# The last two groups of both token mixers in another order, and the first mixer's chunks joined

## The chip, the cores and the metric

The kernel runs on one core of one Trainium2 chip. Its engines are TensorE (PE; its weight loads are listed as PEld), VectorE (DVE), ScalarE (ACT), GpSimd (POOL) and the queue of SyncE (SP), from which most transfers are issued. Each engine works through its own list of instructions in order and waits on semaphores. The metric is the time of one execution in microseconds (us).

## The reference, cut to what matters

The trunk has two layers on 256 tokens of width 1024: SwiGLU feed-forward, token mixer, SwiGLU feed-forward, each between two RMS norms. The mixer of layer 0 is gated linear attention (GLA, 4 heads), that of layer 1 is the Mamba-2 mixer (SSD, 8 groups). All is float32.

```python
def rmsnorm(x, g):
    y = x * lax.rsqrt(mean(x * x, -1) + 1e-6)
    return y * g

for i in range(2):
    x = x + 0.5 * rmsnorm(swiglu(rmsnorm(x, g[0]), ...), g[1])
    h = rmsnorm(x, g[2])
    h = gla_mixer(h, ...) if i == 0 else ssd_mixer(h, ...)
    x = x + rmsnorm(h, g[3])
    x = x + 0.5 * rmsnorm(swiglu(rmsnorm(x, g[4]), ...), g[5])

# gla_mixer, per head, chunks of 64 tokens; b = cumulative log decay in the chunk
scores = tril(einsum(q * exp(b - b_mid), k * exp(b_mid - b)))
o_i    = scores @ v + (q * exp(b)) @ state
state  = state * exp(b_last) + (k * exp(b_last - b)).T @ v
o      = rmsnorm(o per head, g_norm) * silu(r); return o @ w_out

# ssd_mixer, per group: causal conv of 4 taps and silu on x, B, C; chunked scan in the same manner,
y      = (y + d * x) * silu(z); y = rmsnorm(y per group of 256, g_norm); return y @ w_out
```

## The kernel before, in words

**Matrix products.** Each float32 weight is split into a high part, rounded to the format fp32r, and the rest. ScalarE makes the high part (`hi`, and `gate_up_hi` for a quarter of a feed-forward unit, lines 527 and 577), VectorE the rest (`lo`, `gate_up_lo`, lines 891 and 975): 2048 columns on 128 partitions for a mixer's weight slot, 1024 for a quarter. A product is then three TensorE passes. Products of plain float32 tiles (transposes, scores, state) go through TensorE without a split.

**Memory.** Four weight slots (0 to 3) take the transfers; slots 0 and 1 also hold a feed-forward unit's gate and up weights, in four quarters. PSUM has eight banks: 0 to 3 collect the output of the stage (two token tiles of 128 by 1024 columns), A, B, C and E (4 to 7) are working banks.

**A mixer** runs over its groups (heads in GLA) in a software pipeline of three steps, `body(g, proj, scan, outp)` on each engine: *proj* projects group g (P1: features, P2, P3: tokens), *scan* computes group g-1 (rows of keys transposed, scores, state, output, norm), *outp* multiplies the normed output of group g-2 with its rows of `w_out` into banks 0 to 3 (`add_output`, 24 products of 512 columns). The loop runs g = 2 to n-2, and `body(n-1)`, `body(n)` and `body(n+1)` are written out. `body(n)` projects nothing: it scans the last group. `body(n+1)` only adds the last group's output. There the next feed-forward stage's first unit is converted too: all four quarters stand in `body(n-1)`.

**A group's norm** (line 1310 on): ScalarE squares and sums, VectorE computes 1/root in 13 small steps by shift and three Newton iterations (`rsqrt2`, line 900; one more product before and after in GLA), scales `yn` (line 1325), TensorE transposes it (line 1620), ScalarE takes it out of PSUM (line 809) and VectorE its rest (line 1223), and `add_output` can start.

**GLA** has four chunks of 64: three state products on 64 rows (line 1701), four products of the scores (line 1721), three with the states (line 1727), between them a copy and two updates of the state on VectorE (lines 1267 and 1270). `decayed` (line 1136) makes the decayed queries and keys, each by one operation of 256 columns. SSD already works on tiles of 128 tokens.

**The boundary** behind a mixer: each half of the output (512 columns) is squared on ScalarE (line 546) and multiplied with the gains on VectorE (line 927), then the root, the residual update (line 945), TensorE's transposes of x (line 1404) and the first products of the feed-forward stage (line 1362). GpSimd multiplies SSD's rows with their weights (lines 490 to 498).

## Time and profile before

| | us |
|---|---|
| median of 3 runs | 1189.26 |
| lowest and highest run | 1186.78, 1190.22 |
| the profiled execution, its own time | 1189.44 |
| its span, first to last instruction | 1187.7 |
| TensorE busy | 1123.2 (95%) |
| VectorE busy | 738.4 (62%) |
| ScalarE busy | 631.4 (53%) |
| TensorE's mean granted clock | 0.969 of full |

TensorE is busy nearly always. A reader looks for the stretches in which it is not, and for the stretches in which its granted clock is half. GLA lies at 227 to 357 us of the span, SSD at 751 to 995.

### The profile page before, as it was taken

Reading aid. Unit: us, or ns where it says so; the run is one execution under the profiler, and the core shown is the slowest. Engines: PE = TensorE matmul, PEld = TensorE weight load, DVE = VectorE, ACT = ScalarE, POOL = GpSimd, SP = SyncE. Lnnn points to the kernel's source line nnn. Section 1 sums busy time; section 2 is a strip of 40 time slices with the busy share of each in tenths; the row PEclk is TensorE's granted clock in tenths of the full one; section 3 lists DMA queues with packets and bytes.
Section 4 is the critical chain, followed back from the end, with each engine's and each line's share of the span. In section 5 each row is a group of like instructions: output and inputs, shape, how many; then the busy total and the mean of one; then the engine's idle time right before and its main releaser. Section 6 shows DMA issues by size and latency. Waiting matters only on the chain. (4 is left out here: it accounts for less than half of the span.)

```text
span 1187.7 us, 16534 instructions
## 1 busy us (share of the span) xinstructions
PE 1123.2 (95%) x5904; PEld 950.9 (80%) x5904; DVE 738.4 (62%) x1174; ACT 631.4 (53%) x978; POOL 52.2 (4%) x81
## 2 busy tenths in 40 slices
PE   6899999969979999999999997999999969999997
PEld 5688888858848888888888885889999957888886
DVE  4545555756657555557655545698999885655554
ACT  6444445664437444447544445577677746544443
POOL 3000000000000000000000000211211100000000
PEclk9899999989979999999999998899999978999999
DMA  7756554443445655553766534484544504855530
GB/s 244 248 178 211 183 170 133 134 134 115 142 142 175 223 178 176 184 190 118 250 203 198 177 106 137 155 272 144 172 144 143 176 15 147 282 192 177 176 127 35
DMA packets 162877, 199.24 MB, mean 168 GB/s; under 512 B 6372, under 2 KB 145856, under 8 KB 162832
## 3 DMA queue, kind: packets, MB, share of 16 engines
q1 hardware_dynamic: 160144, 190.34, 49.4%
q0 software_dynamic: 2384, 7.72, 1.9%
q8 instruction: 26, 0.43, 0.2%
q10 hardware_dynamic: 304, 0.61, 0.1%
q14 instruction: 19, 0.16, 0.0%
HBM read 197.56 MB, written 1.08 MB: 167 GB/s over the span
## 5 line engine op out<-in xcount | busy, mean ns | idle before, releaser
L1362 PE MATMUL ps<-ws,xT 128*128 128x512 f32 x2160 | 502.3, 391 | 6.2 <-DVE ws L979 6.2
L1362 PEld LDWEIGHTS ps<-ws,xT 128*128 128x128 f32 x2160 | 404.6, 188 | 93.8 <-DVE ws L979 8.0
L1381 PE MATMUL ps<-ws,hT 128*128 128x512 f32 x1344 | 337.8, 402 | 4.0 <-DVE hT L1223 3.9
L1381 PEld LDWEIGHTS ps<-ws,hT 128*128 128x128 f32 x1344 | 253.5, 192 | 59.1 <-issue 6.8
L979 DVE TENSOR_TENSOR ws<-raw,ws 128x1024 fp32r<-128x1024 f32 x180 | 218.3, 1223 | 117.1 <-ACT ws L592 116.9
L897 DVE TENSOR_TENSOR ws<-raw,ws 128x2048 fp32r<-128x2048 f32 x90 | 206.8, 2298 | 99.1 <-ACT ws L532 98.7
L592 ACT ACTIVATE ws<-raw 128x1024 fp32r<-128x1024 f32 x180 | 188.3, 1060 | 145.3 <-PE ps L1362 141.7
L532 ACT ACTIVATE ws<-raw 128x2048 fp32r<-128x2048 f32 x90 | 171.1, 1913 | 58.6 <-PE ps L1381 52.4
L1414 PE MATMUL ps<-xT,ws 128*128 128x256 f32 x960 | 119.3, 284 | 0.3 <-ACT feat L538 0.3
L1414 PEld LDWEIGHTS ps<-xT,ws 128*128 128x128 f32 x960 | 116.4, 192 | 0.9 <-DVE ws L897 0.5
L992 DVE TENSOR_TENSOR hT<-ps,hT 128x256 fp32r<-128x256 f32 x88 | 33.7, 420 | 87.0 <-ACT hT L606 86.9
L1424 PE MATMUL ps<-ws,xT 128*128 128x256 f32 x672 | 87.4, 291 | 0.4 <-ACT ca L538 0.4
L1424 PEld LDWEIGHTS ps<-ws,xT 128*128 128x128 f32 x672 | 84.6, 197 | 2.9 <-issue 2.1
L606 ACT ACTIVATE hT<-ps 128x256 fp32r<-128x256 f32 x88 | 29.5, 381 | 100.4 <-PE ps L1373 100.3
L601 ACT ACTIVATE fm<-ps,sm 128x256 f32<-128x256 f32 x88 | 41.2, 474 | 57.8 <-PE ps L1362 57.8
L985 DVE SCALAR_TENSOR_TENSOR fm<-ps,sm,fm 128x256 f32<-128x256 f32 x88 | 41.8, 483 | 31.9 <-ACT fm L601 31.6
L1156 DVE SCALAR_TENSOR_TENSOR ca<-feat,pcol,ca 128x256 f32<-128x256 f32 x96 | 49.6, 583 | 0.0
L507 POOL DMA_DIRECT2D gpost<-in_norm_gain x5 | 2.8, 556 | 756.1 <-DVE scr L927 756.1
L538 ACT ACTIVATE feat<-ps 128x256 f32<-128x256 f32 x32 | 12.0, 382 | 41.6 <-PE ps L1414 41.3
L927 DVE TENSOR_TENSOR scr<-ps,gpost 128x512 f32<-128x512 f32 x24 | 16.6, 691 | 28.0 <-ACT scr L546 28.0
L969 DVE SCALAR_TENSOR_TENSOR xT<-ps,gcol,xT 128x128 fp32r<-128x128 f32 x96 | 26.6, 343 | 11.6 <-ACT xT L574 11.1
L574 ACT ACTIVATE xT<-ps,gcol 128x128 fp32r<-128x128 f32 x96 | 26.3, 375 | 12.0 <-PE ps L1404 12.0
(196 smaller groups left out, 632.8 us busy)
## 6 DMA issues: line engine op xcount, KB each, us to landing
raw<-in_ffn_w_down SPq DMA_DIRECT2D x88, 512.0 KB, 4.3
raw<-in_ffn_w_gate SPq DMA_DIRECT2D x86, 512.0 KB, 4.0
raw<-in_ffn_w_up SPq DMA_DIRECT2D x86, 512.0 KB, 5.0
raw<-in_ssd_w_in SPq DMA_DIRECT2D x48, 512.0 KB, 4.7
raw<-in_gla_w_in SPq DMA_DIRECT2D x24, 512.0 KB, 4.7
raw<-in_ssd_w_out SPq DMA_DIRECT2D x16, 512.0 KB, 4.2
raw<-in_gla_w_out SPq DMA_DIRECT2D x8, 512.0 KB, 4.8
exps<-cs_rows POOLq DMA_DIRECT2D x8, 512.0 KB, 8.9
```

Source lines behind the costliest of these rows:

```text
L532: act.activation(ws[:, slot, 0, :], raw[:, slot, :], ACT.Copy).then_inc(hi_done[slot], 1)
L592: act.activation(ws[:, 0:2, 0, c], raw[:, 0:2, c], ACT.Copy).then_inc(gu_hi, 1)
L601: act.activation(fm[:, t, :], ps[:, bank + t, 0:UW], ACT.Silu, scale=RPRE[t]).then_inc(silu_g, 1)
L897: return dve.tensor_tensor(ws[:, slot, 1, cols], raw[:, slot, cols], ws[:, slot, 0, cols].bitcast(F32), ALU.subtract)
L979: dve.tensor_tensor(ws[:, 0:2, 1, c], raw[:, 0:2, c], ws[:, 0:2, 0, c].bitcast(F32), ALU.subtract).then_inc(gu_lo, 1)
L985: dve.scalar_tensor_tensor(out=fm[:, 2 + t, :], in0=ps[:, bank + t, UW:2 * UW], scalar=RPRE[t], in1=fm[:, t, :], op0=ALU.mult, op1=ALU.mul ...
L992: dve.tensor_tensor(hT[:, par, :, 1, cs], ps[:, C + t, 0:T].rearrange("p (j n) -> p j n", j=2), hT[:, par, :, 0, cs].bitcast(F32), ALU.sub ...
L1156: ins = dve.scalar_tensor_tensor(out=ca[:, c, :], in0=src, scalar=tap, in1=ca[:, c, :], op0=ALU.mult, op1=ALU.add)
L1362: mm = pe.matmul(ps[:, bank + t, :].rearrange("p (s n) -> p s n", s=2), xT[:, k, a, t * P:(t + 1) * P], ws[:, 0:2, b, k * UW:(k + 1) * UW] ...
L1381: mm = pe.matmul(ps[:, 2 * t + n, :], hT[:, par, j, a, t * P:(t + 1) * P], ws[:, slot, b, off:off + 512], start=(first and j + a + b == 0) ...
L1414: mm = pe.matmul(ps[:, banks + c, 0:T], ws[:, slot, a, off:off + P], xT[:, k, b, :], start=(k == 0 and a + b == 0), stop=(k == KD - 1 and ...
L1424: mm = pe.matmul(ps[:, banks + t, 0:UW], xT[:, k, a, t * P:(t + 1) * P], ws[:, slot, b, k * UW:(k + 1) * UW], start=(k == 0 and a + b == 0 ...
```

## The change

On every engine `body(n-1)`, `body(n)` and `body(n+1)` of both mixers are reordered.

- TensorE: the last group's P3 is cut in two tiles; between them stand the transposed rows and the scores of the last group, which stood in `body(n)`. The first tile's bank stays C, the second's is A, the scores go to B. `add_output` of group n-2 is one piece of 24 products in front of the last transposes, where it was two of 12.
- ScalarE: the four quarters leave `body(n-1)`. Two stand in `body(n)` ahead of the second P3 tile's evacuation, two behind the conversion of the last output weights. The table for Sqrt is loaded in `body(n)`, behind the last Silu, and the last group's root is taken by ScalarE.
- VectorE: the quarters leave `body(n-1)`; three stand behind the last group's transposed rest, the fourth in the boundary. SSD's second convolution stands ahead of the state's copy, and the output weights of group n-2 are converted ahead of the norm (in SSD). The last group's 1/root is a reciprocal of ScalarE's root with one Newton iteration.
- GLA's chunks are joined in all groups: two chunks make a tile of 128 tokens, the decay between them is folded into `decayed` (three operations instead of one for two of the four features), and a group has one state product, two products of the scores on 128 rows and one with the state.

In SSD, TensorE's end before, from the last group's P3 (ws by xT, 256 columns) to the output's products ahead of the transposes of x:

```order
L1424 MATMUL ps<-ws,xT 128x256 x48
L1647 MATMUL ps<-ident,fm 128x128 x4
L1665 MATMUL ps<-ident,fm 128x128
L1668 MATMUL ps<-fm 128x128 x2
L1620 MATMUL ps<-ident,yn 128x128 x4
L1696 MATMUL ps<-xw,scr 128x256
L1712 MATMUL ps<-xdt,wm 128x64 x8
L1716 MATMUL ps<-scr,fm 128x256
L1381 MATMUL ps<-ws,hT 128x512 x12
L1620 MATMUL ps<-ident,yn 128x128 x4
L1381 MATMUL ps<-ws,hT 128x512 x30
```

and now:

```order
L1476 MATMUL ps<-ws,xT 128x256 x24
L1684 MATMUL ps<-ident,fm 128x128 x4
L1693 MATMUL ps<-ident,fm 128x128
L1696 MATMUL ps<-fm 128x128 x2
L1476 MATMUL ps<-ws,xT 128x256 x24
L1674 MATMUL ps<-ident,yn 128x128 x4
L1762 MATMUL ps<-xw,scr 128x256
L1775 MATMUL ps<-xdt,wm 128x64 x8
L1779 MATMUL ps<-scr,fm 128x256
L1433 MATMUL ps<-ws,hT 128x512 x24
L1674 MATMUL ps<-ident,yn 128x128 x4
L1433 MATMUL ps<-ws,hT 128x512 x18
```

The transposed rows of `fm` and the scores stand between two halves of P3, and `add_output` (ws by hT) of group n-2 is whole in front of the last transposes of `yn`; behind them 18 products stand ahead of the transposes of x, where 30 stood.

In SSD, VectorE before, from the state's copy in `body(n-1)`, and then the scaling of `yn` there:

```order
L1247 COPY scr<-ps 128x256
L979 TENSOR_TENSOR ws<-raw,ws 128x2x512 x2
L1153 TENSOR_SCALAR ca<-feat,pcol 128x256 x2
L1156 SCALAR_TENSOR_TENSOR ca<-feat,pcol,ca 128x256 x6
L1288 TENSOR_TENSOR yn<-ps,dx 128x512
L1290 TENSOR_TENSOR vs<-ps,dtv 128x256
L1293 TENSOR_TENSOR yn<-yn,vs 128x256
L1295 TENSOR_TENSOR yn<-yn,zs 128x512
L979 TENSOR_TENSOR ws<-raw,ws 128x2x512 x2
...
L1325 TENSOR_SCALAR yn<-yn,sm 128x256 x2
L897 TENSOR_TENSOR ws<-raw,ws 128x2048
```

and now, from the decayed scores in `body(n-1)`, and then the last scaling and what follows it:

```order
L1311 TENSOR_TENSOR wm<-exps,scr 128x512 x2
L1188 TENSOR_SCALAR ca<-feat,pcol 128x256 x2
L1191 SCALAR_TENSOR_TENSOR ca<-feat,pcol,ca 128x256 x6
L1320 COPY scr<-ps 128x256
L1354 TENSOR_TENSOR yn<-ps,dx 128x512
L1356 TENSOR_TENSOR vs<-ps,dtv 128x256
L1359 TENSOR_TENSOR yn<-yn,vs 128x256
L1361 TENSOR_TENSOR yn<-yn,zs 128x512
L918 TENSOR_TENSOR ws<-raw,ws 128x2048
...
L1275 TENSOR_SCALAR yn<-yn,sm 128x256 x2
L1291 SCALAR_TENSOR_TENSOR hT<-ps,pcol,hT 128x256 x2
L1000 TENSOR_TENSOR ws<-raw,ws 128x2x512 x3
```

The quarters (128x2x512) are gone from between the convolution, the output and its norm; three follow the last transposed rest. The convolution (`ca`) moved ahead of the copy.

In GLA's loop, TensorE's products behind P2 before (`xw`: state, `wm`: scores by values, `fm` and `scr`: queries by states):

```order
L1673 MATMUL ps<-fm 64x64 x4
L1381 MATMUL ps<-ws,hT 128x512 x24
L1701 MATMUL ps<-vs,xw 128x256 x3
L1721 MATMUL ps<-vs,wm 64x256 x4
L1727 MATMUL ps<-scr,fm 64x256 x3
```

and now:

```order
L1701 MATMUL ps<-fm 64x64 x4
L1704 MATMUL ps<-fm 64x64 x2
L1433 MATMUL ps<-ws,hT 128x512 x24
L1766 MATMUL ps<-vs,xw 128x256
L1783 MATMUL ps<-vs,wm 128x256 x2
L1786 MATMUL ps<-scr,fm 128x256
```

Ten products became four, the scores six instead of four.

In the diff `ahead` is `body(n-1)` and `tail` is `body(n)`; `p3_tile(o, t, bank)` evacuates one P3 tile on ScalarE.

```diff
...
-                        act.activation(bcb[:, :], ps[:, C, 0:384], ACT.Copy).then_inc(e_out, 1)
-                    if scan and not proj:
-                        transposed(A)
-                    if isinstance(g, int) and g == n - 1:
-                        for q in range(NQ):
+                        act.activation(bcb[:, :], ps[:, B if tail else C, 0:384], ACT.Copy).then_inc(e_out, 1)
+                    if tail:
+                        for q in range(2):
                             gate_up_hi(gate_units_before(ph + 1), q, ph + 1)
-                    elif proj:
+                        p3_tile(n - 1, 1, A)
+                        if ssd:
+                            gate_silu()
+                        act.activation(DUMMY, EPS_COL[1.0], ACT.Sqrt)
+                        transposed(C)
...
                         hi(*out_unit(g - 1, n, n0))
+                    if tail:
+                        for q in range(2, NQ):
+                            gate_up_hi(gate_units_before(ph + 1), q, ph + 1)
...
+                    if tail:
+                        act.wait_ge(y_sq, 2 * (g - 1 + G) + 2)
+                        for t in range(NT):
+                            act.activation(sm[:, 26 + t:27 + t], sm[:, 8 + t:9 + t], ACT.Sqrt, scale=1.0 if ssd else R2[:, t:t + 1],
+                                           bias=EPS_COL[1.0 / 16]).then_inc(root_y, 1)
...
+                if b < NPH and PHASES[b - 1][0] != "ffn":
+                    gate_up_lo(gate_units_before(b), NQ - 1)
...
+                    near, far, through = (3, 0, 2) if o == 2 else (0, 3, 1)
+                    step.start(part(o, far * CH, near * CH, CH))
+                    part(o, CH, CH, 2 * CH)
+                    step.wait()
+                    dve.tensor_scalar(fm[:, o, near * CH:(near + 1) * CH], fm[:, o, far * CH:(far + 1) * CH],
+                                      edl[:, 0, bass.ds(4 * g + through, 1)], None, ALU.mult).then_inc(feat_done, 1)
...
+                        dve.wait_ge(root_y, 4 if ssd else 2)
+                        step(dve.reciprocal(y, sm[:, 26:28]))
+                        step(dve.tensor_tensor(a, y, y, ALU.mult))
+                        step(dve.tensor_tensor(a, a, mh, ALU.mult))
+                        step(dve.scalar_tensor_tensor(out=y, in0=a, scalar=1.5, in1=y, op0=ALU.add, op1=ALU.mult))
...
+                    if not scan:
+                        for q in range(NQ - 1):
+                            gate_up_lo(gate_units_before(ph + 1), q)
...
-                        for c, (bank, o) in () if ssd else ((0, (E, 0)), (2, (E, 256)), (1, (C, 0))):
...
+                            pe.matmul(ps[:, E, 0:256], xw[:, 0, 0:P], vs[:, 0, :], start=True, stop=True,
+                                      skip_group_check=True).then_inc(upd_mm, 1)
+                        if tail:
+                            pe.wait_ge(p3_out, 2 * (g - 1 + G) + 2)
...
+                            for t in range(NT):
+                                pe.matmul(ps[:, A + t, 0:256], wm[:, t, 0, :], vs[:, t, :], start=True, stop=(t == 0),
                                           skip_group_check=True)
...
+                            pe.wait_ge(state_done, g)
+                            pe.matmul(ps[:, B, 0:256], fm[:, 2, P:2 * P], st[:, 0, :], start=False, stop=True,
+                                      skip_group_check=True).then_inc(off_mm, 1)
+                    if tail:
+                        add_output(n - 2)
+                    if ahead:
+                        split(SLOT_P3, g + n0[SLOT_P3])
+                        pe.wait_ge(state_done, G + g if ssd else g)
+                        token_tiles(SLOT_P3, C, (0,))
+                        pe.wait_ge(feat_done, 4 * (g + G) + 2)
+                        rows(g)
+                        pe.wait_ge(y_out, 2 * (g - 1 + G) + 2)
+                        scores(g, B)
+                        token_tiles(SLOT_P3, A - 1, (1,))
...
```

## Rows read from the trace of the kernel before

**Rows 1.** TensorE's waits: line, releaser: us in total, times, longest.

```profile
PE ps L1620 <- DVE yn L1325: 11.8, 3, 4.7
PE ps L1649 <- DVE fm L1140: 8.6, 1, 8.6
```

**Rows 2.** TensorE in order of time, SSD's end: start us, us, form [idle before].

```profile
950.77 6.09 PE L1424 MATMUL ps<-ws,xT 128*128 128x256 f32 x48
...
964.30 1.11 PE L1620 MATMUL ps<-ident,yn 128*128 128x128 f32 x4 [4.65 <-DVE yn L1325]
...
980.48 0.66 PE L1620 MATMUL ps<-ident,yn 128*128 128x128 f32 x4 [3.38 <-DVE yn L1325]
983.07 9.78 PE L1381 MATMUL ps<-ws,hT 128*128 128x512 f32 x30 [1.93 <-DVE hT L1223]
...
994.94 5.08 PE L1362 MATMUL ps<-ws,xT 128*128 128x512 f32 x21
```

**Rows 3.** Windows 328.1:334.7, 341.7:348.3, 959.5:973.0, 980.0:986.7: length, busy per engine, clock, DMA.

```profile
959.50:973.00 13.50, 6.20 (x27) 5.27 (x25) 9.07 (x19) 3.31 (x5) 2.75 (x4) 0.57 0.00 1
...
sum 33.40, PE 18.21 PEld 13.40 DVE 17.25 ACT 11.31 POOL 2.75; mean PE 4.55 PEld 3.35 DVE 4.31 ACT 2.83 POOL 0.69
```

**Rows 4.** TensorE in order of time, SSD's loop undisturbed.

```profile
862.28 5.73 PE L1381 MATMUL ps<-ws,hT 128*128 128x512 f32 x24
867.85 0.59 PE L1696 MATMUL ps<-xw,scr 128*128 128x256 f32 x2
868.28 1.89 PE L1712 MATMUL ps<-xdt,wm 128*128 128x64 f32 x16
```

**Rows 5.** TensorE in order of time, GLA's third group and the stage's end.

```profile
317.24 1.13 PE L1701 MATMUL ps<-vs,xw 64*128 64x256 f32 x6
...
320.63 6.01 PE L1424 MATMUL ps<-ws,xT 128*128 128x256 f32 x48
...
357.43 5.09 PE L1362 MATMUL ps<-ws,xT 128*128 128x512 f32 x21
```

**Rows 6.** The page's costliest groups: busy us, mean ns | idle before.

```profile
L979 DVE TENSOR_TENSOR ws<-raw,ws 128x1024 fp32r<-128x1024 f32 x180 | 218.3, 1223 | 117.1 <-ACT ws L592 116.9
L897 DVE TENSOR_TENSOR ws<-raw,ws 128x2048 fp32r<-128x2048 f32 x90 | 206.8, 2298 | 99.1 <-ACT ws L532 98.7
L592 ACT ACTIVATE ws<-raw 128x1024 fp32r<-128x1024 f32 x180 | 188.3, 1060 | 145.3 <-PE ps L1362 141.7
```

**Rows 7.** VectorE in order of time: loop norm, then the last two groups.

```profile
932.15 0.16 DVE L903 TENSOR_SCALAR sm<-sm 128x2 f32<-128x2 f32 x1
...
934.58 0.61 DVE L1325 TENSOR_SCALAR yn<-yn,sm 128x256 f32<-128x256 f32 x2
...
954.45 0.69 DVE L1288 TENSOR_TENSOR yn<-ps,dx 128x512 f32<-128x512 f32 x1
...
959.03 0.16 DVE L903 TENSOR_SCALAR sm<-sm 128x2 f32<-128x2 f32 x1
...
963.63 0.62 DVE L1325 TENSOR_SCALAR yn<-yn,sm 128x256 f32<-128x256 f32 x2 [0.28 <-DVE sm L912]
```

**Rows 8.** GpSimd in order of time, the last group.

```profile
959.81 0.61 POOL L490 TENSOR_TENSOR xw<-scr,dtv 128x256 f32<-128x256 f32 x1 [19.08 <-ACT scr L818]
```

**Rows 9.** VectorE in order of time: GLA's state and features, the boundary's residual update.

```profile
318.93 1.06 DVE L1270 SCALAR_TENSOR_TENSOR scr<-scr,edl,ps 128x256 f32<-128x256 f32 x2
319.92 1.09 DVE L1140 SCALAR_TENSOR_TENSOR fm<-ca,exps 128x256 f32<-128x256 f32 x3
...
990.65 1.42 DVE L945 SCALAR_TENSOR_TENSOR xres<-scr,sm,xres 128x512 f32<-128x512 f32 x2
```

**Rows 10.** ScalarE in order of time behind GLA's last group.

```profile
345.24 1.28 ACT L614 ACT_TABLE_LOAD   x1
346.54 0.20 ACT L614 ACTIVATE sm<-sm 128x1 f32<-128x1 f32 x1
```

**Rows 11.** The page's DMA issues: KB each, median us to landing.

```profile
raw<-in_ffn_w_up SPq DMA_DIRECT2D x86, 512.0 KB, 5.0
```

More of the change, by code:

```diff
@@ L36 @@
 QW = UNIT // NQ
-CONST_IDENT, CONST_EPS, CONST_ALL = 2, 5, 12
+CONST_IDENT, CONST_EPS, CONST_ALL = 2, 6, 12
 SSD_WEIGHTS = 4
-SSD_STEPS, GLA_STEPS = 15, 15
+SSD_STEPS, GLA_STEPS = 15, 17
 MASKED_FIRST = 2
@@ L466, in _ @@
             step(pool.memset(ones[:, :], 1.0))
-            for c in range(2):
-                r = slice(c * CH, (c + 1) * CH)
-                step(pool.tensor_copy(mask[r, :], tri[r, r]))
+            step(pool.memset(wm[CH:P, :, 0, 0:CH], 0.0))
             step(pool.memset(feat[:, :, 0:CONV - 1], 0.0))
@@ L788, in body, with gate_silu @@
                     first = isinstance(g, int) and g == 1
-                    if scan:
+                    ahead = isinstance(g, int) and g == n - 1
+                    tail = scan and not proj
+                    def gate_silu():
                         if not first:
@@ L1215, in body @@
                     first = isinstance(g, int) and g == 1
+                    ahead = isinstance(g, int) and g == n - 1
+                    tail = scan and not proj
                     c0 = g * 2 + 2 * G
@@ L1248, in body @@
                         else:
-                            mk = mask[:, :].rearrange("p (t i) -> p t i", t=1).broadcast_to([P, NT, CH])
                             dve.wait_ge(e_mm, g - 1 + G + 1)
-                            dve.tensor_tensor(wm[:, :, 0, 0:CH], ps[:, C, 0:P].rearrange("p (t i) -> p t i", t=2), mk,
-                                              ALU.mult).then_inc(w_done, 2)
-                    if scan and not proj:
-                        transposed(A)
-                    if isinstance(g, int) and g == n - 1:
-                        for q in range(2):
-                            gate_up_lo(gate_units_before(ph + 1), q)
-                    elif proj:
+                            scores = ps[:, B if tail else C, 0:2 * P].rearrange("p (t i) -> p t i", t=2)
@@ new lines, in body @@
+                            past = tri[:, CH:P].rearrange("p (t i) -> p t i", t=1).broadcast_to([P, NT, CH])
+                            dve.tensor_tensor(wm[:, :, 0, CH:P], scores[:, :, CH:P], past, ALU.mult).then_inc(w_done, 1)
+                            past = tri[0:CH, 0:CH].rearrange("p (t i) -> p t i", t=1).broadcast_to([CH, NT, CH])
+                            dve.tensor_tensor(wm[0:CH, :, 0, 0:CH], scores[0:CH, :, 0:CH], past, ALU.mult).then_inc(w_done, 1)
+                    if tail and not ssd:
+                        transposed(C)
@@ L1605, in body @@
                     last = not proj and not scan
+                    ahead = isinstance(g, int) and g == n - 1
+                    tail = scan and not proj
                     c0 = g * 2 + 2 * G
@@ L1679, in body @@
                         add_output(n - 1, (0,), True)
-                        add_output(n - 2, (1,))
                         add_output(n - 1, (1,), True)
-                    if scan and not proj:
-                        transpose_rows(A)
+                    if tail:
+                        pe.wait_ge(p3_out, 2 * (g - 1 + G) + 1)
+                        transpose_rows(C)
                     if scan:
```

186 lines of the change are left out of this document (99 added, 87 removed).

## The prediction

> **What bounds the kernel now.** Start with the busy shares: TensorE 95%, the others far below. So TensorE's list sets the time, and only three things can shorten it: fewer or shorter products, fewer waits, fewer stretches at half clock. The view of TensorE's waits comes next. The reader is to see that two of its rows are nearly half of all that TensorE waits: the transposes of `yn` behind the norm, 11.8 us in 3 waits, and the transposes in front of GLA's first scan, 8.6 us once [rows 1]. Then the list in order of time shows where the first sits: at SSD's end. From the last P3 (950.77) to the feed-forward stage's first product (994.94) 44.2 us pass, with waits of 4.65, 3.38 and 1.93 us [rows 2], of which some 6.1 us are P3 itself. GLA's end looks the same: 317.24 to 357.43, 40.2 us [rows 5]. Last the windows: in the four stretches where the waits lie, the granted clock is 0.57 in the longest, that is mostly the lower level of 1.2 GHz, and TensorE is busy 18.21 us in the 33.4 [rows 3]. The same four transposes take 1.11 us at 964.30 and 0.66 at 980.48 [rows 2]: what is half clocked takes nearly twice as long. These two ends are the place of the change.
>
> **SSD's end, walked step by step.** Up to 950.77 TensorE does the same work in the same order.
> - P3's first tile takes half of 6.09 us, to 953.8; transposed rows and scores about 0.9 (a guess from neighbours of 128 columns), the second tile to 957.6.
> - VectorE: the convolution ran ahead of the copy, in time in which it waited, and two quarters of 1.22 us [rows 6] are gone. So the output starts not at 954.45 but when TensorE's product is there, 950.8: 3.7 us earlier, done at 953.2. Then a conversion of 2.3 us [rows 6], and the norm starts at 955.4 instead of 959.03.
> - The norm. In the loop it takes 934.58 + 0.61 - 932.15 = 3.0 us; in the last groups 963.63 + 0.62 - 959.03 = 5.2 us [rows 7]. The difference of 2.2 us begins with GpSimd's multiplies at 959.81 [rows 8], and VectorE's small steps stretch while they run. In the new order GpSimd gets its rows at about 955.1, so its multiplies again fall on the norm. I take 5.1: done at 960.5. TensorE waits 2.9 us, where it waited 4.65. Without the overlap it would be 0.8.
> - The decayed scores (1.3) come behind the norm on VectorE, to 961.8; then the scores' product 1.9 and the state's 0.4, to 964.0; `add_output` in one piece, 5.7 [rows 4], to 969.7.
> - Beside it: output to gated output 2.4 us from 963.8, squares 0.8, roots and five small steps 1.5, two scalings 0.6, and the conversion of 2.3 us in between, partly hiding squares: 970.0. TensorE waits 0.3 where it waited 3.38. The remaining transposes, ScalarE's copy and VectorE's rest take 983.07 - 980.48 = 2.6 us [rows 2] as before: 972.6.
> - Then 12 + 6 products to 976.9. Here is the new wait. The residual update of the first tile must be done before TensorE transposes x. Before, 30 products (7.2 us at full clock, 9.78 as granted) covered it; now only 6 stand between the tile's end at 975.5 and the transposes. Squares, gains, root chain, half an update of 1.42 us [rows 9] and the three quarters of 3.7 us in front of the gains put x at 979.0. Wait: 2.1 us. Transposes and 6 products end at 981.7.
> - 994.94 - 981.7 = **13.2 us saved** at full clock. The fourth quarter (1.2 us) falls where VectorE waits for the second tile's squares; I cost it at 0, or 1.2 if that cover is gone.
>
> **GLA's end.** The same list from 317.24: products 1.7 instead of 3.4 (below), first tile, rows and scores, second tile to 325.6. The norm (3.4 us here) no longer has quarters ahead and is done at 324.7, so TensorE doesn't wait for it. New waits come: ScalarE loads the Sqrt table (1.28 us [rows 10]) behind the second tile's evacuation, so the transposed copy starts at 327.7, not 326.1; and the masked scores stand behind a conversion on VectorE, 327.6. TensorE waits 1.5 us there and 1.0 for the state copied behind the rest of `hT`. `add_output` ends at 336.05; ScalarE converts two quarters of 1.06 us [rows 6] ahead of the squares, and the norm is still done at 335.7. Then 2.4, 12 + 6 products, 2.5 for x, and the end at 347.7. 357.43 - 347.7 = **9.7 us saved** at full clock.
>
> **GLA's loop.** Ten products took 320.63 - 317.24 = 3.39 us [rows 5]. The new four are of the form 128x256 on 128 rows, whose start-to-start is 868.28 - 867.85 = 0.43 us [rows 4]: 1.72. That is 1.7 less per group; the two added score products (64x64) about pay for the dropped transpose. Groups 1 and 2 give **3.4** (bounds 2.0 and 4.0: the first group also waits on VectorE), group 3 is in the walk above. VectorE loses two state updates of 0.53 and gains steps in `decayed`: three features took 1.09, 0.36 each [rows 9]; three pieces with a wait cost at least three small ones of 0.16 [rows 7] and at most three of 0.36, so +0.15 to +0.75 each. I take +0.3. In the loop TensorE covers that; at GLA's start two of these stand ahead of the products that already wait 8.6 us [rows 1]: **-0.6** (0.3 to 1.5). The masks' replacement on GpSimd lies in the first microseconds: 0.
>
> **The clock.** Both walks assume 2.4 GHz. In the four windows TensorE was busy 18.21 us [rows 3], so the lower level cost up to 9.1. New waits of 1 to 3 us remain at five places, so the clock will still fall. Lower bound 0, upper 12 (a denser list at half clock loses more per us). I take **-6**, nearer to before, since the 2.9, 2.1 and 2.6 us waits resemble those that led to a fall.
>
> **Sum.** 13.2 + 9.7 + 3.4 - 0.6 - 6 = 19.7. The profiled execution took 1189.44 (span 1187.7, 1.7 outside); the median of the runs is 1189.26, the same within 0.02%. 1189.44 - 19.7 = **1169.7 us**.
>
> **A rule weighed against the change.** GLA's new table load lies on the path. In the trace it takes 1.28 us, from 345.24, and the next instruction starts at 346.54, 0.02 behind it [rows 10]; 1.28 is what the walk holds. The Trainium skill, ScalarE: Activation LUTs, "What ACT_TABLE_LOAD costs", adds to each switch of tables a drain of about 1.4 us. By that rule the gain would be 1.4 us smaller, 1171.1; this trace shows no such gap.
>
> **Rivals.**
> - *The clock stays up.* If the closed waits keep it at 2.4 GHz nearly everywhere, the 6 us come back: 1164. For it: 3.38 and half of 4.65 us of waits go at SSD's end; against: waits remain in both ends.
> - *New waits take more.* The residual update that lost its cover (18 instead of 30 products), the fourth quarter, the Sqrt load and the norm that still meets GpSimd each cost more than walked, about 1.5 us each in two stages, and the clock costs 9 instead of 6. Then 10 to 11 us are left: 1179. For it: each is a chain over three engines that I pieced together; against: each is short.
> - *The waits only move.* If the reordered ends gave nothing but the freed products and the first wait, 3.4 + 1.7 + 3 = 8 minus new ones of 4: 1185. Against: the norm's earlier start rests on order alone.
> - *Slower: the next stage starves.* The loads of the second feed-forward unit into slots 0 and 1 wait for the first unit's converted quarters, and these now end at about 348.8 in GLA's walk (347.7 and the fourth quarter's 1.2), where they stood in `body(n-1)`. With 5.0 us to land [rows 11] the second unit is there at 354, and ScalarE wants it when TensorE has read the first unit's first quarters, some 10 us behind 347.7. From 3 us more it decides: if the late transfers queued so that each stage's start waits over 10 us, both together eat the gain: 1192. Nothing in the trace shows such a landing time.
>
> **How the numbers follow.** Forecast (1166 to 1174) 0.45; clock stays up 0.2; new waits take more 0.24; waits only move 0.06; starving 0.05. The likeliest is 1169.7. The range for 8 in 10 takes most of the second and third: 1161 to 1179. A difference of 0.3% (3.6 us) is about what a measurement of this kernel can tell from none. Faster by more than that: 0.92 (all but the last and part of the fourth); within: 0.04; slower: 0.04.
>
> **What would show it.** Right: the wait of the `yn` transposes falls from 11.8 to about 3.2 us, all in SSD; the time from SSD's last P3 to the first feed-forward product is 31 us plus the clock's loss; GLA's loop step falls by 1.7 per group; the transposes of x wait about 2 us at both ends. Wrong: the norm done before 959 (no meeting with GpSimd), waits of over 4 us ahead of the transposes of x, half clock over more than 20 us in the two ends, or waits for raw weights in the first units.

## The result, and the profile of the changed kernel

The changed kernel takes 1168.41 us (median of 4 runs, 1166.21 to 1170.95), the kernel before 1189.74 in the same session (1186.78 to 1190.90): 0.9821 of the time, 95% interval 0.9804 to 0.9838, so 21.3 us less. The prediction said 1169.7. The profiled execution is the shortest of the four, 1166.21 us with a span of 1164.5 (the span runs from the first instruction to the last); its span is 23.2 us shorter than the one before, and that is the sum to be split.

TensorE's waits, largest and new ones (line, releaser: us in total, times, longest), beside [rows 1]:

```profile
PE ps L1686 <- DVE fm L1176: 9.0, 1, 9.0
...
PE ps L1433 <- DVE hT L1291: 3.9, 2, 1.9
...
PE ps L1456 <- DVE xres L966: 3.2, 2, 1.6
PE ps L1674 <- DVE yn L1275: 2.4, 1, 2.4
PE ps L1786 <- DVE scr L1336: 2.4, 2, 1.3
```

The transposes of `yn` waited 11.8 us in three places and now wait 2.4 in one. New are 3.2 us ahead of the transposes of x, in two waits. The wait at GLA's start is 9.0 instead of 8.6.

TensorE in order of time at SSD's end, beside [rows 2]:

```profile
937.47 3.21 PE L1476 MATMUL ps<-ws,xT 128*128 128x256 f32 x24
...
946.98 0.63 PE L1674 MATMUL ps<-ident,yn 128*128 128x128 f32 x4 [2.44 <-DVE yn L1275]
947.44 0.60 PE L1762 MATMUL ps<-xw,scr 128*128 128x256 f32 x2
948.09 3.68 PE L1775 MATMUL ps<-xdt,wm 128*128 128x64 f32 x16
951.56 1.17 PE L1779 MATMUL ps<-scr,fm 128*128 128x256 f32 x2
952.16 7.13 PE L1433 MATMUL ps<-ws,hT 128*128 128x512 f32 x24
959.13 0.60 PE L1674 MATMUL ps<-ident,yn 128*128 128x128 f32 x4
961.66 5.95 PE L1433 MATMUL ps<-ws,hT 128*128 128x512 f32 x18 [1.93 <-DVE hT L1291]
969.17 1.32 PE L1456 MATMUL ps<-ident,xres 128*128 128x128 f32 x8 [1.56 <-DVE xres L966]
...
971.70 5.11 PE L1414 MATMUL ps<-ws,xT 128*128 128x512 f32 x21
```

From the last P3 to the feed-forward stage's first product 34.23 us pass where 44.17 did: 9.94 gained. Of these 8.3 are waits: before there were five, the three of [rows 2] and these two, 14.21 us together, and now three of 5.93 us.

```profile
958.47 0.63 PE L1647 MATMUL ps<-ident,fm 128*128 128x128 f32 x4 [1.60 <-ACT zf L538]
...
968.92 3.65 PE L1712 MATMUL ps<-xdt,wm 128*128 128x64 f32 x16 [2.65 <-DVE hT L1223]
```

The 16 products at 948.09 take 3.68 us, against 1.89 at full clock [rows 4], and the 18 at 961.66 take 5.95: behind the waits of 2.44 and 1.93 us TensorE runs at half clock. At GLA's end the kernel before had these four waits, 8.24 us in all:

```profile
327.29 0.41 PE L1649 MATMUL ps<-ident,fm 128*128 128x128 f32 x2 [0.66 <-ACT vs L538]
...
330.60 2.04 PE L1701 MATMUL ps<-vs,xw 64*128 64x256 f32 x6 [1.83 <-DVE wm L1251]
...
343.42 0.93 PE L1620 MATMUL ps<-ident,yn 128*128 128x128 f32 x4 [3.82 <-DVE yn L1325]
346.28 9.06 PE L1381 MATMUL ps<-ws,hT 128*128 128x512 f32 x30 [1.93 <-DVE hT L1223]
```

And now, beside [rows 5]:

```profile
314.38 0.59 PE L1766 MATMUL ps<-vs,xw 128*128 128x256 f32 x2
...
322.77 0.60 PE L1674 MATMUL ps<-ident,yn 128*128 128x128 f32 x4
324.38 0.67 PE L1766 MATMUL ps<-vs,xw 128*128 128x256 f32 x2 [1.01 <-DVE wm L1327]
...
326.98 0.70 PE L1786 MATMUL ps<-scr,fm 128*128 128x256 f32 x2 [1.07 <-DVE scr L1336]
...
335.53 4.36 PE L1433 MATMUL ps<-ws,hT 128*128 128x512 f32 x18 [1.93 <-DVE hT L1291]
341.53 1.32 PE L1456 MATMUL ps<-ident,xres 128*128 128x128 f32 x8 [1.64 <-DVE xres L966]
...
344.07 2.21 PE L1414 MATMUL ps<-ws,xT 128*128 128x512 f32 x9
```

29.69 us instead of 40.19: 10.50 gained, and here the 18 products take 4.36 us, full clock. The waits explain only 2.6 of it (5.65 us now). The other 7.9 are shorter products: some 3.4 are the joined chunks' in the third and the last group (an estimate, 3.39 us for ten products before, 1.54 and 1.88 for four now), and most of the rest is half clock that is gone (the 30 products behind 346.28 took 9.06 us, 7.2 at full clock). The granted clock of this stretch was 0.83 before and is 1.00 now; SSD's end had 0.77 and has 0.85.

The third group starts at 314.38 instead of 317.24, 2.86 earlier: 2.64 of it lie between GLA's first products and there, and 0.22 ahead of them, where TensorE's list is the same in both kernels. 9.94 + 10.50 + 2.86 = 23.3 of the 23.2 us. The two windows (length, busy us per engine, TensorE's clock, DMA), GLA's end and SSD's:

```profile
314.40:344.00 29.60, 23.95 (x142) 19.97 (x141) 23.64 (x67) 18.48 (x40) 0.00 (x0) 1.00 0.31 107
```
```profile
937.50:971.70 34.20, 28.21 (x143) 23.89 (x142) 26.58 (x58) 18.88 (x43) 2.85 (x4) 0.85 0.26 93
```

VectorE's norm in SSD's last full group (first and last step), and GpSimd beside it:

```profile
941.98 0.58 DVE L924 TENSOR_SCALAR sm<-sm 128x2 f32<-128x2 f32 x1
...
946.22 0.62 DVE L1275 TENSOR_SCALAR yn<-yn,sm 128x256 f32<-128x256 f32 x2
```
```profile
941.83 0.71 POOL L488 TENSOR_TENSOR xw<-scr,dtv 128x256 f32<-128x256 f32 x1 [14.41 <-ACT scr L827]
942.50 1.04 POOL L491 TENSOR_TENSOR xdt<-scr,dtv 128x512 f32<-128x512 f32 x1
```

The norm still meets GpSimd's multiplies and takes 4.86 us, not the loop's 3.0 [rows 7].

### The profile page after: what moved, and what is told of

It reads as the page before. It is cut to its first block, busy times and chain, and to the rows that moved or that the text cites. A ratio compares the mean times of both kernels' runs of the same rounds, so it can differ in the third digit from the quotient of the medians.

```text
span 1164.5 us, 16442 instructions
## 1 busy us (share of the span) xinstructions
PE 1111.0 (95%) x5868; PEld 947.5 (81%) x5868; DVE 733.4 (63%) x1170; ACT 631.9 (54%) x984; POOL 54.1 (5%) x81
## 4 chain that ended last, share of the span: by engine, by line
PE 88%; DVE 6%; ACT 3%; issue 1%; DMA 1%; SPq 0%; DVEq 0%; ACTq 0%
PE ps L1414 41%; PE ps L1433 25%; PE ps L1466 8%; PE ps L1476 6%; PE ps L1425 2%; PE ps L1775 1%; DVE ws L918 1%; DVE ws L1000 1%; PE ps L1456 1%; ACT ws L530 1%; DMA raw<-in_ffn_w_down 1%; PE ps L1584 1%; DVE xT L990 1%; DVE xres L966 0%; DVE ca L1191 0%
## 5 line engine op out<-in xcount | busy, mean ns | idle before, releaser
L1425 PE MATMUL ps<-ident,fm 128*128 128x128 f32 x176 | 27.6, 276 | 3.2 <-DVE fm L1006 3.2
```

Of the source, the lines that this page charges most:

```text
L1425: mm = pe.transpose(ps[:, C + t, j * P:(j + 1) * P], fm[:, 2 + t, j * P:(j + 1) * P], ident[:, :])
```

## The experiments

Twelve kernels, each timed beside the kernel before (medians 1189.47 to 1189.74). Single runs of one kernel spread over 2 to 7 us and the intervals of the ratios are 1.5 to 2.6 us to each side, so a difference of less than some 2 us between two of these medians says little; the traces decide there. "SSD's end" and "GLA's end" are the two stretches above.

Whole traces can't be compared either. TensorE reaches GLA's first product with `xdt` at 228.53 us in one of these traces and at 233.51 in another (229.95 before, 229.73 in the changed kernel), although its list is the same to there; the granted clock of the first 60 us was 0.94 and 0.83 in these two. The time from GLA's end to SSD's last P3, the same list too, goes from 590.64 to 594.72 us (593.34 and 593.40). Behind SSD's end all of them take 192.7 to 192.8. So only the two ends are compared below.

**The joined chunks alone.** In the kernel before:

```diff
-                        for c, (bank, o) in () if ssd else ...
+                            for to, keys, queries in ((CH, 3, 1), (3 * CH, 2, 0)):
+                                mm = pe.matmul(ps[0:CH, C, to:to + CH], fm[:, 3, keys * CH:(keys + 1) * CH], ...
+                            pe.matmul(ps[:, E, 0:256], xw[:, 0, 0:P], vs[:, 0, :], start=True, stop=True, ...
```

> The kernel before with one part of the change alone: GLA's chunks joined (one state product per group of 256 tokens, one output product more per tile, no transpose of the second feature tile). Theory: the joined chunks give back 1.5 to 1.7 us in each of two groups of the loop, 1.3 in the last group at full clock and somewhat more where that ran at half clock, less 0.6 at GLA's start: 4.5 to 6 us, about 1184. Then the order of the last groups and the norm hold the other 15 to 17 us. Rival: in the kernel before, the added VectorE steps of the features are not covered and the freed TensorE time turns into waits at the norm: 0 to 2 us, 1187 to 1190. A second rival, that the clock alone reacts (a denser list keeps it up in GLA's end): over 7 us, under 1182.

1184.65 us, ratio 0.9947 (0.9934 to 0.9960): 5.1 us less. GLA's end shrank from 40.19 to 36.75, more than its share of products, SSD's hardly (44.17 to 43.46). The waits at `yn` stayed, in four places:

```profile
PE ps L1621 <- DVE yn L1326: 11.6, 4, 4.4
```

So the join gives about 5 us, and the other 16 are the order's by subtraction: no run has the order without the join.

**The quarters back in the last full group.**

```diff
+                    if ahead:
+                        for q in range(NQ):
+                            gate_up_hi(gate_units_before(ph + 1), q, ph + 1)
...
+                    if ahead:
+                        for q in range(2):
+                            gate_up_lo(gate_units_before(ph + 1), q)
...
+                    if ahead:
+                        for q in range(2, NQ):
+                            gate_up_lo(gate_units_before(ph + 1), q)
...
-                        for q in range(NQ - 1):
-                            gate_up_lo(gate_units_before(ph + 1), q)
```

> The changed kernel with one part undone: the feed-forward weights' quarters are converted in the last full group again, two on VectorE and all four on ScalarE ahead of the norm, as before the change. Theory: in SSD's end the norm starts about 2.4 us later (two quarters of 1.22 us), and all of it reaches TensorE, since it waits 2.4 us there already; GLA's norm has 1.2 us of slack. ScalarE loses the quarters behind the last norm and the boundary gains a little. Together +3 to +5 us with what the longer wait costs in clock: 1171.5 to 1173.5. Rival: the norm meets GpSimd's multiplies in the present order and takes 4.9 instead of 3.0 us; a later norm misses them, so only 0.5 us is lost: 1169. In that case the norm's duration in the trace is near 3 us. Second rival: the loads behind the quarters start earlier and something is gained, below 1167.

1171.42 us, 0.9839 (0.9826 to 0.9852): 3.0 more than the changed kernel. TensorE's waits:

```profile
PE ps L1673 <- DVE yn L1271: 5.0, 3, 3.7
```

SSD's end is 37.29 us (939.59 to 976.88), 3.06 longer; the norm takes 4.8 us again, so the first rival is out. GLA's end is 32.18 us, 2.5 longer: the norm is late there too (1.13), the masked scores are (1.96 instead of 1.01), and the products behind run at half clock. The two ends together are 5.55 us longer in the traces; the medians differ by 3.0, and the intervals of the ratios just overlap (the changed kernel's ends at 0.9838). The conversions did stand in front of the norm. It is the only piece of the order that, undone alone, cost a measurable time: the next two runs undo one each and their medians don't differ. The remaining 13 us or so (the rows and scores brought ahead into `body(n-1)`, the convolution ahead of the copy, `add_output` in one piece) rest on the traces' waits and clock; no run takes them apart.

**The last root on VectorE.**

```diff
-                    if tail:
-                        act.wait_ge(y_sq, 2 * (g - 1 + G) + 2)
...
-                        norm(g, tail)
+                        norm(g, False)
```

> The changed kernel with the last norm's root computed on VectorE by steps, as in the loop, and no root on ScalarE; the load of the Sqrt table stays where it is. Theory: the last norm is on the path with little slack (SSD: yn ready at 958.05, TensorE there at 959.13; GLA: 332.4 against 333.0). The chain on VectorE is about 1.5 to 1.9 us longer than root, reciprocal and four steps, so each end loses 0.5 to 1.3 us: +1 to +2.5 us, 1169.5 to 1171. Rival: VectorE's chain is hidden behind the second conversion or ScalarE's squares, as TensorE waited for another thing there: no change, 1168.4 within 0.5. The wait of the transposes of yn in the third place tells them apart.

1168.56 us, 0.9812 (0.9798 to 0.9827): no difference in time. The waits do appear, 0.53 us in SSD's end and 0.88 in GLA's:

```profile
961.27 0.66 PE L1669 MATMUL ps<-ident,yn 128*128 128x128 f32 x4 [0.53 <-DVE yn L1270]
963.86 4.36 PE L1428 MATMUL ps<-ws,hT 128*128 128x512 f32 x18 [1.93 <-DVE hT L1286]
```

In SSD the 18 products behind run at full clock here (4.36 against 5.95 us), which outweighs the wait: 33.34 instead of 34.23. In GLA's end it is the other way round:

```profile
338.36 5.95 PE L1428 MATMUL ps<-ws,hT 128*128 128x512 f32 x18 [1.93 <-DVE hT L1286]
```

GLA's end is 32.29 us where it was 29.69, 0.88 for the wait and 1.6 for the clock. The step is worth up to 1.4 us of waits, about as much as one such change of the clock (1.6).

**P3 in one piece ahead of rows and scores.**

```diff
                         token_tiles(SLOT_P3, C, (0,))
+                        pe.wait_ge(y_out, 2 * (g - 1 + G) + 2)
+                        token_tiles(SLOT_P3, A - 1, (1,))
                         pe.wait_ge(feat_done, 4 * (g + G) + 2)
                         rows(g)
-                        pe.wait_ge(y_out, 2 * (g - 1 + G) + 2)
                         scores(g, B)
-                        token_tiles(SLOT_P3, A - 1, (1,))
```

> The changed kernel with both tiles of P3 in one piece in the last full group of SSD and GLA, and the transposed rows and scores behind them instead of between them. Theory: rows and scores come 3 us later, so ScalarE's token copy, GpSimd's multiplies and the masked scores on VectorE come later as well; TensorE gains nothing ahead of the norm, and the scores' product waits about 1 to 2 us longer in each end: +1.5 to +4 us, 1170 to 1172.5. Rival: GpSimd's multiplies then fall behind VectorE's norm, which takes 3.0 instead of 4.9 us, and TensorE's wait of 2.4 us at the first yn transposes shrinks: -1 to -2 us, 1166.5 to 1167.5. The norm's duration and the wait ahead of the state product tell them apart.

1168.67 us, 0.9830 (0.9816 to 0.9844): not to be told from the changed kernel. Both mechanisms are there. In SSD's end GpSimd now falls behind the norm, which takes 3.0 us (942.16 to 945.2), and the first wait shrinks; two others take its place:

```profile
945.35 0.63 PE L1674 MATMUL ps<-ident,yn 128*128 128x128 f32 x4 [0.61 <-DVE yn L1275]
947.27 0.67 PE L1762 MATMUL ps<-xw,scr 128*128 128x256 f32 x2 [1.29 <-POOL xdt L491]
...
951.70 1.22 PE L1779 MATMUL ps<-scr,fm 128*128 128x256 f32 x2 [0.59 <-DVE scr L1320]
```

0.61 + 1.29 + 0.59 = 2.49 for 2.44. SSD's end is 34.14 us, as long as before this edit. GLA's end is 32.48, 2.8 longer: the state's copy comes later (2.33 us of wait in place of 1.07), as the theory had it for each end, and the last 18 products run at half clock (5.97).

**Zeros in the waits.** They add 0 to a bank and change no result.

```diff
+                        for _ in range(count):
+                            pe.matmul(ps[:, 3, :].rearrange("p (o n) -> p o n", o=4), zr[:, :], zeros, start=False, ...
...
+                        fill(8 if ssd else 3)
                         pe.wait_ge(p3_out, 2 * (g - 1 + G) + 1)
...
                         transpose_rows(C)
+                        if last:
+                            fill(6)
...
+                                fill(5)
                                 x_transposed(ph + 1, 0)
```

> The changed kernel with products of zeros added in TensorE's waits at both ends of the mixers: 3 (GLA) or 8 (SSD) ahead of the first yn transposes of the last part, 6 behind the last yn transposes, 5 ahead of the transposes of x. They add zeros into a bank of PSUM with the form 128x512 of the output products, so each takes 0.24 us at full clock. Theory: after SSD's waits TensorE runs for some 7 and 3 us at the lower level of 1.2 GHz, which costs about 3.3 us in SSD's end in the trace of the changed kernel; zeros in the waits keep the level up and this comes back: -2 to -3.5 us, 1165 to 1166.5, with granted clock 1.0 in SSD's end. Rival: the level falls for another reason than TensorE's pause, or the zeros reach beyond the waits and push the path: no gain or +1 us.

1163.95 us, 0.9779 (0.9764 to 0.9795): 4.5 less than the changed kernel, more than the theory's 3.5. SSD's end:

```profile
947.94 2.01 PE L1682 MATMUL ps<-zr 128*128 128x512 f32 x8
950.55 0.63 PE L1674 MATMUL ps<-ident,yn 128*128 128x128 f32 x4 [0.60 <-DVE yn L1275]
...
951.66 2.00 PE L1786 MATMUL ps<-xdt,wm 128*128 128x64 f32 x16
...
953.79 5.84 PE L1433 MATMUL ps<-ws,hT 128*128 128x512 f32 x24
959.83 0.66 PE L1674 MATMUL ps<-ident,yn 128*128 128x128 f32 x4 [0.20 <-DVE yn L1275]
...
962.42 4.35 PE L1433 MATMUL ps<-ws,hT 128*128 128x512 f32 x18 [0.55 <-DVE hT L1291]
```
```profile
941.10:970.90 29.80, 27.90 (x162) 23.13 (x161) 26.32 (x58) 18.85 (x43) 2.85 (x4) 1.00 0.30 106
```

The norm ends no earlier (9.37 us behind the start of P3 in both), the other engines do the same, and yet the stretch is 29.92 us instead of 34.23: 3.68 becomes 2.00, 7.13 becomes 5.84, 5.95 becomes 4.35. A wait of 0.20 us at the last transposes takes a little back, and 4.31 us are what half clock cost in SSD's end. GLA's end is 29.71 us against 29.69, as it was at full clock already. The Trainium skill, TensorE: Matmul & The Clock Gate, "What's actually happening", says that the clock depends on how busy the array has been lately, and the trace agrees: the clock was 1.00 with the waits filled, 0.85 without. It isn't an accident of one run: in SSD's end the clock is 1.00 in all three kernels with zeros, and 0.85 to 0.95 in the nine with the new order and no zeros.

**Six output products moved behind the last transposes.**

```diff
-                        add_output(n - 2)
+                        add_output(n - 2, (0,))
+                        down_half(out_unit(n - 2, n, n0)[0], 0, 1, 0)
...
                         transpose_rows(C)
+                        if last:
+                            down_half(out_unit(n - 2, n, n0)[0], 0, 1, 1)
```

> The changed kernel with 6 of the 24 output products of the group before the last moved behind the last yn transposes in both mixers, where TensorE waits 1.93 us for hT. Theory: each of these waits is filled with 1.45 us of products; in front, yn becomes ready 1.1 us (SSD) and 0.6 us (GLA) ahead of TensorE's arrival, so 0.35 and 0.9 us are lost again to a new wait at the transposes: -1.1 and -0.6, together about -1.5 us, 1166.5 to 1167.5. Rival: the wait only moves to the transposes of yn and of x (the end hangs on VectorE's chain, not on TensorE's list): 1168 to 1169. The sum of the waits at yn, hT and xres tells them apart.

1164.42 us, 0.9786 (0.9771 to 0.9801): 4.0 less, more than either expectation. The waits at `hT` fall from 1.93 to 0.55 us; in SSD's end (31.70 us, 2.5 less) that also keeps the last 18 products at full clock, 4.37 us. GLA's end is 29.24, where a wait of 0.69 at `yn` came. The 16 and the first 18 products behind SSD's wait of 2.44 us still run mostly at half clock (3.59 and 5.87 us; 2.00 and 4.47 in the run with both edits below).

**Norm ahead of the conversion.**

```diff
-                        act.activation(DUMMY, EPS_COL[1.0], ACT.Sqrt)
                         transposed(C)
+                        act.activation(DUMMY, EPS_COL[1.0], ACT.Sqrt)
...
                             if tail:
+                                lo(*out_unit(g - 2, n, n0))
                                 transposed(C)
...
-                    if ssd and scan and not first and (ahead or tail):
+                    if ssd and tail:
                         lo(*out_unit(g - 1, n, n0))
...
-                    if scan and proj and not (ssd and ahead):
+                    if scan and proj and not ahead:
```

> The changed kernel with three steps in another order at both ends: VectorE normalises ahead of the conversion of the output weights (2.29 us) and masks or decays the scores right behind it, and ScalarE loads the Sqrt table (1.28 us) behind its copy of the transposed rows, not in front of it. Theory: in SSD the norm starts at the squares, 1.1 us earlier, GpSimd's multiplies still fall on most of it, and TensorE's 2.44 us at the first yn transposes become 1 to 1.5; in GLA the two waits of 1.01 and 1.07 us ahead of the state product and the off product go down to 0.8 together. Together -2 to -3 us with a little from the clock: 1165.5 to 1166.5. Rival: the last norm becomes late instead, as its output waits behind the moved conversion: waits at the third yn transposes of 1 us or more, and the time stays at 1168.

1166.82 us, 0.9799 (0.9782 to 0.9817). In SSD 2.44 became 1.45 and 1.32, so the waits moved; in GLA they went from 1.01 + 1.07 to 0.87, and 0.85 came at the last `yn`. The median is 1.6 less, which the spread doesn't separate from none. But SSD's end is 31.67 us, 2.6 less, although its waits grew by 0.3: the products behind them, 3.68 and 7.13 us in the changed kernel, ran at full clock in this trace:

```profile
951.13 2.00 PE L1777 MATMUL ps<-xdt,wm 128*128 128x64 f32 x16
...
954.80 5.83 PE L1435 MATMUL ps<-ws,hT 128*128 128x512 f32 x24
```

GLA's end is 30.49, 0.8 more, with its last 18 products at half clock (5.95). Both sides were half right.

**The same, with GpSimd held back.**

```diff
+                if g == SSD_G:
+                    pool.wait_ge(yn_done, 2 * (g - 2 + G) + 2)
```

> The order of the run before (norm ahead of the conversion, table load behind the copy) and in SSD's last group GpSimd's multiplies held back until the norm is done. Theory: without GpSimd at work beside it the norm takes 3.0 us as in the loop, not 4.8, is done ahead of TensorE's arrival, and its wait is 0; the state product instead waits for GpSimd's first two multiplies (0.71 and 1.04 us) about 0.7 to 1.3 us. Against the run before: -0.3 to -0.8 us, 1165 to 1166. Rival: what stretches the norm is not GpSimd, then it takes 4.8 us again and the multiplies come later still: +1.5 us or more, 1167.5 to 1168.5.

1166.55 us, 0.9800 (0.9785 to 0.9816), the same as before it. The norm takes 3.0 us (944.20 to 947.16), so GpSimd is what stretches it; TensorE doesn't wait for it, but 1.57 us for GpSimd. And now VectorE's next steps and GpSimd stretch each other:

```profile
948.79 3.12 DVE L920 TENSOR_TENSOR ws<-raw,ws 128x2048 fp32r<-128x2048 f32 x1
```
```profile
949.73 3.23 POOL L498 TENSOR_TENSOR dx<-scr,hb 128x256 f32<-128x256 f32 x2
```

These took 2.29 and 1.18 us in the changed kernel. In this order the collision moved and didn't go away.

**One quarter ahead of the last `hT`.**

```diff
+                    if not scan:
+                        gate_up_lo(gate_units_before(ph + 1), 0)
                     if outp and (proj or not scan):
                         transposed(C)
```

> The changed kernel with VectorE's first converted quarter (1.2 us) moved from behind to in front of the last copy of hT, into the time in which VectorE waits for ScalarE there (2.06 us in GLA, 2.58 in SSD). Theory: in GLA the three quarters (3.48 us) hold the gained output back by 0.8 us behind the squares, and TensorE's 1.64 us at the transposes of x shrink to about 0.9; in SSD the gained output already waits 0.42 us for ScalarE, so nothing changes: -0.6 to -0.8 us, 1167.7. Rival: the x transposes hang on the root chain and the squares alone, no change in either wait (both 1.5 to 1.7 us): 1168.4.

1168.05 us, 0.9817 (0.9796 to 0.9838). The waits at x are 1.50 and 1.54 us, where 1.64 and 1.56 were: the gained output now waits for ScalarE's squares. GLA's 18 products ran at half clock in this trace (5.96), which gives the quarters more time; the run with the table load moved, with the same half clock and no moved quarter, waits 1.52. At full clock the last two runs below compare: from the first of the 18 products to the transposes of x 5.95 us pass with the quarter in front and 5.99 without. The chain of squares, root and update sets the wait, not the quarters: the rival holds.

**The table load behind the copy.**

```diff
-                        act.activation(DUMMY, EPS_COL[1.0], ACT.Sqrt)
                         transposed(C)
+                        act.activation(DUMMY, EPS_COL[1.0], ACT.Sqrt)
```

> The changed kernel with one line moved: ScalarE loads the Sqrt table (1.28 us) behind its copy of the transposed rows instead of in front of it. Theory: in GLA the copy comes 1.3 us earlier, with it the state copy on VectorE, and TensorE's 1.07 us ahead of the off product go to 0; in SSD TensorE's yn transposes are later than the table load, so nothing: -1 us, 1167.4. Rival: the state copy then waits for the state product, which itself waits 1.01 us for the masked scores; 0.87 of the wait stays, as in the run with the three steps in another order: -0.2 us, 1168.2.

1167.13 us, 0.9818 (0.9799 to 0.9836). The wait of 1.07 us goes to 0, as the theory had it, but the load now delays ScalarE's conversion and with it the last norm:

```profile
327.08 5.82 PE L1433 MATMUL ps<-ws,hT 128*128 128x512 f32 x24
333.65 0.66 PE L1674 MATMUL ps<-ident,yn 128*128 128x128 f32 x4 [0.75 <-DVE yn L1275]
```

So the load costs 0.3 us where it stands. The median is what the theory named, 1.3 less than the changed kernel's, but the trace doesn't show 1 us gained: GLA's end is 30.80, with its last 18 products at half clock (5.98).

**Moved products and zeros together, and everything.** The edits above, joined.

> The changed kernel with both edits that paid: 6 output products moved behind the last yn transposes, and products of zeros in the remaining waits (3 or 8 ahead of the first yn transposes of the last part, 5 ahead of the transposes of x). Theory: the moved products save 1.4 us at hT in each end less a new wait at yn, the zeros keep TensorE at 2.4 GHz; in SSD's end 29.9 us with zeros alone become 28.8, in GLA's 29.7 become 29.2: 1162 to 1163. Rival: both work on the same loss (a wait that is filled with products is a pause less, and the clock came up by that already), so together they give what the better one gives, 1164.

1162.55 us, 0.9776 (0.9754 to 0.9798), the best median of all: 5.9 less than the changed kernel and 26.9 less than before. SSD's end is 29.94 us, the same as with zeros alone (a wait of 1.56 at `yn` replaces the 1.4 saved), GLA's 29.23, the same as with moved products alone. So by the traces the two edits work on one loss, as the rival has it; the median lies in the theory's range, but its lead over either alone (1.4 and 1.9 us) is within the spread.

> The run with moved products and zeros, and in addition the table load behind the copy and the first quarter in front of the last hT. Theory: 0.2 to 1 us (load) and 0.7 us (quarter) more in GLA's end, nothing in SSD's: 1161 to 1162. Rival: with the six products moved, the last norm is the late one in GLA, and the quarter in front of hT pushes hT itself in SSD, where less time is left: no change or +0.5 us against the run with moved products and zeros, 1162.5 to 1163.5.

1164.61 us, 0.9801 (0.9782 to 0.9821): not better. GLA's end is 29.94 us and SSD's 30.11, 0.7 and 0.2 more than in the run before. In GLA the last `yn` is late (0.69 there):

```profile
331.36 0.66 PE L1676 MATMUL ps<-ident,yn 128*128 128x128 f32 x4 [2.22 <-DVE yn L1275]
```

## Why the prediction was right, step by step

- **What bounds it.** Right: all of the gain lies in TensorE's list at the two ends and in GLA's loop, 23.3 of 23.2 us, and nothing downstream moved (593.34 and 593.40 us between the ends, 192.76 and 192.80 behind). The exact match is in part luck, as the stretch between the ends differs by up to 4 us from trace to trace.
- **SSD's end, 13.2 at full clock.** In the zeros' run, all at full clock, it lasts 29.92 us: 44.17 - 29.92 = 14.25, so the walk was 1.05 too short of the gain. Its waits were 2.44 (walked 2.9), 0.20 at the last transposes (0.3) and, with full clock ahead of it, 1.63 at x (2.1; the run with moved products). These three make up the 1.05. The norm met GpSimd as foreseen: 4.86 for 5.1. The new wait for the residual update is real.
- **GLA's end, 9.7.** 10.5. The waits were 1.01 (1.5), 1.07 (1.0), 1.93 (inside the 2.4) and 1.64 (2.5). The last is the mis-sized term: from the first of the 18 products to the transposes of x I walked 6.8 us and 6.00 passed, which is the whole 0.8. I let the quarters stand in front of the gains for the whole 3.7 us, but they take 3.48 and mostly lie beside the squares (moving one away changed this time by 0.04 at full clock).
- **Loop and start, 3.4 - 0.6 = 2.8.** 3.20 less 0.56 is 2.64, and 0.22 lie ahead of GLA, where nothing changed. The products of the second group took 289.86 - 288.32 = 1.54 us (walked 1.72). At the start 0.34 us are more wait for `fm` and 0.22 stand behind it.
- **The clock, -6.** In the profiled run -4.3, all in SSD's end. It was priced as a share of 9.1 us from four windows, and these leave out the 30 products behind each `hT` wait, 9.78 and 9.06 us for 7.2 at full clock, so the 9.1 was no upper bound of what the clock cost before. That run's GLA end was at full clock by luck: of nine kernels with the new order and no zeros, six had half-clocked products there (window clock 0.94 or 0.95), five of them at the last 18 products, where it costs 1.6 us. With that the term is -4.3 to -5.9. It is one thing that can put the median 2.2 us above the profiled run; the stretches ahead of GLA and between the ends, which differ by more, are another, and the other runs have no trace to tell.
- **The sum.** In the profiled run every term gave more than forecast (the loop's here less the start's): 1.05 + 0.8 + 0.06 + 1.7 = 3.6 us, 23.3 for 19.7. By the medians it is 21.3 for 19.7. That the median is so near to 1169.7 is thus partly luck; the mechanism and the places are right, the sizes within 1.1 us for each walk.
- **The rule weighed.** The new table load took 1.28 us and the next instruction began 0.02 us behind it, with no gap ahead of it either:

```profile
323.46 1.28 ACT L845 ACT_TABLE_LOAD   x1
324.76 0.20 ACT L845 ACTIVATE sm<-sm 128x1 f32<-128x1 f32 x1
```

  The drain of 1.4 us (the Trainium skill, ScalarE: Activation LUTs, "What ACT_TABLE_LOAD costs") isn't seen; the measurement decides, and the sum without it was right. Nor is it seen at the two loads of an SSD group: at 910.77 us, 0.01 behind the end of the instruction ahead, 1.28 us, the next one 0.02 behind.
- **The rivals.** The clock did not stay up by itself (1164). When it was made to, the time was 1163.95; that case had worked out the same from walks 1.9 us too short, so the match is in part luck: the medians also hold what the rest of the kernel does. The new waits did not take more than walked (1179). The waits did not only move (1185): the order gave 16 us beside the joined chunks' 5. No stage starved: behind both ends TensorE takes as long as before. What remains open is why the half-clocked stretches fall in GLA's end in some kernels and not in others with the same waits.

## What to carry to other kernels

Walk the critical engine's list in order of time with the releasing chains beside it: two walks over three engines came within 1.05 and 0.8 us. Price the clock as a term of its own, from products of one form at both levels. When the waits that remain can't be removed, fill them: moving real products into them, or adding products of zeros, gave 4 us here, while five reorderings (four of the other engines, one of TensorE's P3) moved waits of 1 to 2.5 us from one place to the next and gave at most 1.9 us by the median, which the spread doesn't separate from none. Compare single traces only over the stretch that the edit touches: the rest of this kernel differs by 4 to 5 us from one trace to the next.

## What the hardware showed that was not expected

- Zeros gain time. 19 idle products of 0.24 us in SSD's waits, and 14 in GLA's, took 4.5 us off, because what follows runs at 2.4 instead of 1.2 GHz.
- A wait of 1.93 us was followed by half-clocked products in one run (5.95 us for 18) and by full-clocked ones in another (4.36) of nearly the same list. So a single profile gives this term only to 1.6 us for each such place.
- The longest wait alone doesn't tell it either. Behind one wait of 2.44 us the products ran at half clock in all five kernels that left it as it was; behind 1.45 and 1.32 us (norm ahead of the conversion) they ran at full clock; behind 0.61 and 1.29 us (P3 in one piece) and behind 1.57 us (GpSimd held back) at half.
- VectorE's smallest steps can take four times as long beside GpSimd: two steps of 128x1 took 1.54 us in place of 0.35 in the run with the norm ahead of the conversion, while GpSimd's multiply of 128x512 lost nothing (1.04 us). With GpSimd held back it was the other way round for two multiplies of 128x256, 3.23 us in place of 1.18. The Trainium skill, SBUF — State Buffer, "SBUF: two separate sides", calls the ports that the two share an exclusive lock that also steps with two SBUF inputs take; the traces agree that the two slow each other and that either can be the one that is stretched. That one holds the ports for a whole instruction no run here shows.
